# Two decoder blocks on one Trainium2 core: the modulation's matrix-vector product moves from TensorE to ScalarE and accumulating transfers, and the recurrence runs on two half buffers

## The reference, cut to what matters

```
c_act = jax.nn.silu(c)                                  # [1, 1024]
for l in range(2):
    mod = c_act @ w_ada[l] + b_ada[l]                   # w_ada[l]: [1024, 6144], 24 MB each
    sh_m, sc_m, gt_m, sh_f, sc_f, gt_f = jnp.split(mod, 6, axis=-1)
    h = rms_norm(x, g_mix[l]) * (1.0 + sc_m[:, None]) + sh_m[:, None]
    ...
```

## Time and profile before

| | us |
|---|---|
| median of 3 runs | 3211.62 (3207.85 to 3217.34) |
| the profiled execution, its own time | 3216.43 |
| its span in the profile | 3214.3 |
| TensorE busy | 2807.8 (87%) |
| VectorE busy | 1462.0 (45%) |
| ScalarE busy | 877.2 (27%) |
| GpSimd busy | 120.4 (4%) |

### The profile page before, as it was taken

The page is one execution under the profiler, slowest core; times in us unless marked ns, Lnnn a source line. Parts: engine busy times, 40 slices in busy tenths (PEclk is TensorE's granted clock), DMA queues, the critical chain, the costliest instruction groups (busy, mean ns, idle before and its releaser), DMA issues.

```text
span 3214.3 us, 48264 instructions
## 1 busy us (share of the span) xinstructions
PE 2807.8 (87%) x21116; PEld 2057.9 (64%) x21116; DVE 1462.0 (45%) x2707; ACT 877.2 (27%) x1416; POOL 120.4 (4%) x199
## 2 busy tenths in 40 slices
PE   6898989868896877875798899999998888999999
PEld 5686767646573332321676667888876666778887
DVE  5545444467453110102565646434455665554433
ACT  3312212132430000001233353322223334433221
POOL 0010101010000000000000000000000000000000
PEclk9999999978997998997899999999999999999999
DMA  4353534332128999997233332333332342323332
GB/s 145 115 173 100 166 100 149 97 124 107 47 91 354 428 427 428 427 428 289 68 86 102 70 118 86 92 98 94 97 84 82 91 87 86 105 80 97 99 98 79
DMA packets 151816, 489.57 MB, mean 152 GB/s; under 512 B 13232, under 2 KB 41488, under 8 KB 139184
## 3 DMA queue, kind: packets, MB, share of 16 engines
q1 hardware_dynamic: 112256, 362.37, 31.5%
q0 software_dynamic: 26384, 97.32, 9.2%
q10 hardware_dynamic: 12960, 26.74, 2.6%
HBM read 456.49 MB, written 29.90 MB: 151 GB/s over the span
## 4 chain that ended last, share of the span: by engine, by line
PE 67%; DVE 14%; DMA 12%; ACT 5%; issue 2%; SPq 0%; POOL 0%; DVEq 0%; ACTq 0%; POOLq 0%
PE psum L154 64%; DMA wslot<-in_w_up 4%; DMA wslot<-in_w_gate 3%; DMA wslot<-in_w_down 3%; PE psum L157 3%; DVE halfL L163 2%; DVE sc__235 L193 1%; ACT halfH L160 1%; DVE m L190 1%; DVE slot L163 1%; DVE a20S L178 1%; DVE a21S L178 1%; ACT a1S L160 1%; DVE US L163 1%; DMA ada<-in_w_ada 0%
## 5 line engine op out<-in xcount | busy, mean ns | idle before, releaser
L163 DVE TENSOR_TENSOR halfL<-ring,halfH 128x1024 fp32r<-128x1024 f32 x302 | 367.5, 1221 | 684.6 <-ACT halfH L160 684.5
L160 ACT ACTIVATE halfH<-ring 128x1024 fp32r<-128x1024 f32 x302 | 316.5, 1053 | 808.4 <-PE psum L154 808.2
L154 PE MATMUL psum<-hH,halfH 128*128 128x512 f32 x1200 | 486.3, 405 | 9.7 <-DVE halfL L163 9.6
L154 PE MATMUL psum<-hL,halfH 128*128 128x512 f32 x1200 | 473.4, 394 | 0.0
L154 PE MATMUL psum<-hH,halfL 128*128 128x512 f32 x1200 | 472.3, 394 | 0.0
L154 PE MATMUL psum<-wslot,XT 128*64 128x512 f32 x1024 | 258.8, 664 | 73.7 <-DMA wslot<-in_w_gate 42.7
L154 PEld LDWEIGHTS psum<-hH,halfH 128*128 128x128 f32 x1200 | 228.5, 190 | 83.9 <-issue 23.4
L154 PEld LDWEIGHTS psum<-hH,halfL 128*128 128x128 f32 x1200 | 228.5, 190 | 49.6
L154 PEld LDWEIGHTS psum<-hL,halfH 128*128 128x128 f32 x1200 | 229.1, 191 | 44.6
L154 PEld LDWEIGHTS psum<-wslot,XT 128*64 128x64 f32 x1024 | 90.3, 152 | 241.3 <-issue 235.5
L154 PE MATMUL psum<-halfH,hH 128*128 128x512 f32 (+2 forms) x576 | 219.8, 382 | 11.8 <-DVE halfL L163 8.4
(11 more groups left out here) (446 smaller groups left out, 3909.9 us busy)
## 6 DMA issues: line engine op xcount, KB each, us to landing
wslot<-in_w_gate SPq DMA_DIRECT2D x32, 2048.0 KB, 30.0
wslot<-in_w_up SPq DMA_DIRECT2D x32, 2048.0 KB, 28.9
wslot<-in_w_down SPq DMA_DIRECT2D x32, 2048.0 KB, 31.0
ring<-in_w_in SPq DMA_DIRECT2D x120, 512.0 KB, 3.8
ada<-in_w_ada POOLq DMA_DIRECT2D x96, 512.0 KB, 4.2
ring<-in_w_gu SPq DMA_DIRECT2D x88, 512.0 KB, 3.6
ring<-in_w_down SPq DMA_DIRECT2D x44, 512.0 KB, 3.8
gate_rows<-stage ACTq DMA_DIRECT2D x48, 256.0 KB, 2.1
```

Source lines behind the costliest of these rows:

```text
L154: return self.e.matmul(*a, **k)
L160: return self.e.activation(*a, **k)
L163: return self.e.tensor_tensor(*a, **k)
```

## The change

- A weight tile of the modulation is scaled by ScalarE (step `scaled`): row p times `cact[p, k]`. The first of a group (k = 0) goes to `ada_sum` (128 x 1024), the others stay in place.
- GpSimd issues for each of the seven other tiles of a group a transfer that adds the tile to `ada_sum` (84 in all). It waits for the last addition to have landed, issues load n + 2, waits for `scaled` n, and issues addition n. There are three buffers for the tiles.
- TensorE does only the sum over the partitions of the finished group: eight matmuls with a 128 x 128 piece of `ada_sum` as weights and one column of ones, which give `mods` in columns at once. ScalarE's copies to `arow` and the turning go.
- The steps stand elsewhere: per group eight `scaled`, an empty one and one `ada` (120 slots), one slot after each prep other than 1 to 4 and one at each loop step (35 slots a pair). The last group ends at prep 18 of pair 3.
- Two of the three tile buffers lie in the third half buffer. So the recurrence's woven products have two half buffers, splits go one tile ahead, and the first loads of the modulation wait for the last tile before the woven ones.
- The loads of `Zh` and the two gains move from GpSimd's queue to SyncE's, behind the loads of the woven tiles.

```diff
+    half_of, half_before = [], []
+    for n in range(len(tiles)):
+        half_of.append(n % 2 if FIRST_WOVEN <= n <= LAST_WOVEN else n % NH)
+        half_before.append(max([m for m in range(n) if half_of[m] == half_of[n]], default=None))
...
-    ada_in = [rk(f"ada{i}", 1024) for i in range(2)]
+    ada_sum, ada_in = rk("ada_sum", 1024), [rk("ada0", 1024)]
+    ada_in += [sb(f"ada{1 + i}", AT_HALF + 4096 + 1024 * i, 1024) for i in range(2)]
...
+    def ada_steps():
+        for g in range(12):
+            for k in range(8):
+                yield [("scaled", 8 * g + k)]
+            yield []
+            yield [("ada", g)]
...
-                if n_ada < 108:
-                    yield "ada", n_ada // 9, n_ada % 9
-                    n_ada += 1
+                if not 1 <= i < 5:
+                    yield from next(ada, [])
...
                 yield from next(woven, [])
+                yield from next(ada, [])
...
-        def rw_ada(g, k):
...
+        def rw_ada(g):
             b = bank(ADA_BANK)
+            clear(ADA_BANK)
+            pe.wait_ge(*at("ada_sum", 8 * g + 7))
+            for c in range(8):
+                i = pe.matmul(b[:, c:c + 1], ada_sum[:, c * 128:(c + 1) * 128], K("ones", 0, 1), start=True, stop=True)
+            i.then_inc(*up("ada_pe", "ada", g))
...
-                split_to(WOVEN[n][2].tiles[ti][0] + 2, LAST_WOVEN)
+                split_to(WOVEN[n][2].tiles[ti][0] + 1, LAST_WOVEN)
...
+        def rw_scaled(n):
+            ac.wait_ge(*at("cact"))
+            ac.wait_ge(*at("ada_in", n))
+            if n % 8 == 0 and n:
+                ac.wait_ge(*at("ada", n // 8 - 1))
+            ac.activation(ada_in[n % 3] if n % 8 else ada_sum, ada_in[n % 3], COPY,
+                          scale=cact[:, n % 8:n % 8 + 1]).then_inc(*up("ada_act", "scaled", n))
...
+        po.wait_ge(*at("tile", FIRST_WOVEN - 1))
+        for n in range(3):
+            ada_load(n)
         for n in range(96):
...
+            if n:
+                po.wait_ge(*(at("ada_sum", n - 1) if (n - 1) % 8 else at("scaled", n - 1)))
+                if n + 2 < 96:
+                    ada_load(n + 2)
+            po.wait_ge(*at("scaled", n))
+            if n % 8:
+                po.dma_start(ada_sum, ada_in[n % 3], accum_op=AD).then_inc(*landed("ada_sum", "ada_sum", n))
...
+        sp.wait_ge(*at("tile", LAST_WOVEN))
+        for i, who in enumerate(("q", "k")):
+            for ci in range(2):
+                for j in range(4):
+                    sp.wait_ge(*at("kept", who, ci, j))
+            sp.dma_start(Zh[who], z_rows.rearrange("(t p) n -> p t n", p=128)[:, :, 768 * i:768 * i + 768]
+                         ).then_inc(*landed(f"z_{who}", "z_in", who))
```

More of the change, by code:

```diff
@@ L273, in program @@
     t_pi = small("t_pi", 4, dt=I32)
-    arow = small("arow", 256)
     g8 = small("g8", 5)
@@ L325, in program @@
              for ci, ch in enumerate(chs)]
-    LAST_WOVEN = len(tiles) - 1
+    FIRST_WOVEN, LAST_WOVEN = G_q[0].tiles[0][0], len(tiles) - 1
     def merge_chunks(branches, wo):
@@ L589, in recurrence_order @@
     def recurrence_order():
-        n_ada, woven, heads = 0, woven_steps(), list(A1_HEADS)
+        woven, heads, ada = woven_steps(), list(A1_HEADS), ada_steps()
         for pr in range(4):
@@ L617, in recurrence_order @@
                 yield "normed", pr
-        assert not heads
+        assert not heads and next(ada, None) is None
     BETWEEN = {**{1 + i: ("norming", 3, i) for i in range(9)}, 12: ("gated", 3), 14: ("turned", 3)}
@@ L721, in gemm_bank @@
             n, k0, nk = ch.tiles[ti]
-            H, L = tile_view(halfH[n % NH], n), tile_view(halfL[n % NH], n)
+            H, L = tile_view(halfH[half_of[n]], n), tile_view(halfL[half_of[n]], n)
             n_out = ch.w // 128 if stay == "weights" else 4
@@ L1223, in split_to @@
                 ac.wait_ge(*at("tile_in", m))
-                if m >= NH:
-                    ac.wait_ge(*at("tile", m - NH))
-                ac.activation(tile_view(halfH[m % NH], m), tile_view(ring[m % NW], m),
+                if half_before[m] is not None:
+                    ac.wait_ge(*at("tile", half_before[m]))
+                ac.activation(tile_view(halfH[half_of[m]], m), tile_view(ring[m % NW], m),
                               COPY).then_inc(*up("split_act", "hsplit", m))
@@ L1541, in scalar_program @@
         ac.wait_ge(*at("us", 11))
-        handlers = {"head": rw_head, "prep": rw_prep, "normed": rw_normed, "turned": rw_turned, "ada": rw_ada,
+        handlers = {"head": rw_head, "prep": rw_prep, "normed": rw_normed, "turned": rw_turned, "scaled": rw_scaled,
                     "gemm": rw_gemm, "spill": rw_spill, "square": a1_square, "root": a1_root, "turn": a1_turn,
@@ L1576, in split_to @@
                 ve.wait_ge(*at("hsplit", m))
-                ve.tensor_tensor(tile_view(halfL[m % NH], m), tile_view(ring[m % NW], m),
-                                 tile_view(halfH[m % NH], m).bitcast(F32), SU).then_inc(*up("split_dve", "lsplit", m))
+                ve.tensor_tensor(tile_view(halfL[half_of[m]], m), tile_view(ring[m % NW], m),
+                                 tile_view(halfH[half_of[m]], m).bitcast(F32), SU).then_inc(*up("split_dve", "lsplit", m))
                 done[0] += 1
@@ L1834, in a1_turn, with rw_ada @@
             turned_out("a1", who, j, GEMM_BANKS[j % 4], *((qT, g8[:, 0:1]) if who == "q" else (kT, col("gqk", 1))))
[L1836 to L1841, removed]
+        def rw_ada(g):
+            ve.wait_ge(*at("ada", g))
+            ve.tensor_copy(mods[:, 8 * g:8 * g + 8], bank(ADA_BANK)[:, 0:8]).then_inc(*up("ada_dve", "mods", g))
         H_ = "hd_dve"
@@ L2302, in vector_program @@
         ve.wait_ge(*at("consts"))
-        ve.memset(arow, 0.0).then_inc(*up("ada_dve"))
         ve.memset(U[:, :, 0:514:513], 0.0).then_inc(*up(R_))
@@ L2371, in pool_program, with ada_load @@
         po.wait_ge(*at("n1", "turn", 7))
-        for n in range(96):
[L2373 to L2389, removed]
+        def ada_load(n):
+            L, part, k = n // 48, n // 8 % 6, n % 8
+            po.dma_start(ada_in[n % 3], T["w_ada_2"][L, k * 128:(k + 1) * 128,
+                                                     part * 1024:(part + 1) * 1024]).then_inc(*landed(f"ada{n % 3}",
+                                                                                                      "ada_in", n))
+        po.wait_ge(*at("tile", FIRST_WOVEN - 1))
+        for n in range(3):
+            ada_load(n)
+        for n in range(96):
+            if n:
[5 more added lines that the diff above has]
+                po.dma_start(ada_sum, ada_in[n % 3], accum_op=AD).then_inc(*landed("ada_sum", "ada_sum", n))
         po.wait_ge(*at(("a1", "q"), "turn", 5))
@@ L2502, in sync_program @@
             load(n)
+        sp.wait_ge(*at("tile", LAST_WOVEN))
[5 more added lines that the diff above has]
+                         ).then_inc(*landed(f"z_{who}", "z_in", who))
+        sp.dma_start(gqk_["q"], T["q_norm_g"].to_broadcast([128, 64])).then_inc(*landed("gqk"))
+        sp.dma_start(gqk_["k"], T["k_norm_g"].to_broadcast([128, 64])).then_inc(*landed("gqk", "gqk_in"))
         sp.wait_ge(*at("a1", "s", A1.n - 1))
```

## The result

The changed kernel takes 3463.7 us (median of 4 runs, 3460.2 to 3467.6), the one before 3210.0 us in the same comparison (4 runs): ratio 1.0786, 95% interval 1.0765 to 1.0808. It is slower by 7.9%; I had forecast slower, by 1.0%, in a range that ended at 3362.

What follows compares the result with a forecast made beforehand. The prediction took TensorE's order to bound the recurrence before, and the chain of additions after: its end at 758 us against 726 makes 32 us later, 3211.6 + 32 = 3243.6, said as 3244 us, range 3165 to 3362.

Steps and rivals of the forecast that it cites:

- the sum of the chain: GpSimd's additions in the recurrence: 137 + 12 x 44 + 84 + 9 = 758 us when the last group is summed.
- the landing X: Time from an adding transfer's issue on GpSimd's queue to its landing, taken as 5.0 us; break-even 4.6.
- the load ahead: What is left of the load in front of an addition in GpSimd's queue: 1.2 - 0.54 = 0.7 us.
- the restart: Between two groups of additions: TensorE's sum 2.1, two scalings 2.1 and signals 0.3, together 4.5 us.
- the holes: Stretches almost without slots from a loop's end to the next pair's prep 5: 28 us idle at each of three, 84.
- case A: Forecast, chance 0.45: the additions pace the recurrence, X between 4.7 and 6, 3220 to 3328 us, likeliest 3244.
- case C: Rival, chance 0.15: additions much slower than two reads, X from 6 on; 3370 us at 6.5, TensorE idle, clock lower.
- 84 links: Successive additions into one buffer, each 0.54 issue of the load, 5.0 landing and 0.1 to wake: 5.65 us.
- The wake: GpSimd's delay after each addition has landed, before its next instruction: about 0.1 us a link.
- The hidden gain: If every new transfer were hidden: 33 us less on TensorE plus 18 in pair 3 and waits, 51 us.
- The rule: Skill-based estimate of an addition's landing, 2.0 + 1.05 MB / 436 GB/s = 4.4 us; not adopted, sum 50 us lower.

## Why the prediction was wrong

The mechanism was right, and the sizes of its terms were not. The step that failed is the sum of the chain: first the landing X, in it the part for the load ahead (0.7 us taken, 1.8 measured), then the restart and the holes. The chain of additions paces the recurrence, TensorE waits at the sums and ScalarE at the scalings, and GpSimd's waits end by transfers. In sign and in cause this was case A. By its landing of 6.4 us it falls into case C (X from 6 on), and C's signs came too: TensorE idle for a third of the stretch and a lower granted clock. But C's reason was an addition that is slow by itself, and by itself it landed in 4.6 us. In size it was worse than the sum gives even at the X that was measured: 32 + 84 x (6.4 - 5.0) makes 150 us, and it was 254. I went through the chain of the changed kernel from 137 us to the end of its last sum at 975 us, by the terms of my sum, which ended at 758:

| | predicted | measured | difference |
|---|---|---|---|
| 84 links | 5.65 us each, 475 | 7.3 on average, 611 | +136 |
| restarts | 12 of 4.5 us, 54 | ten from 6.3 to 12.0, in sum 85, and the last sum, 4 | +35 |
| without an open link | 93 us | start 28, in pair 1 28, into pair 2 58, others 24 | +45 |

The 58 holds the eleventh restart, which fell into that hole.

**The landing.** X = 5.0 was put together from 3.1 for a copy, 1.2 for the second operand and 0.7 for the load ahead. The runs gave 3.1 for a copy with no load just ahead, 1.5 more for an addition in the same place, and 1.8 more with the load ahead. So the copy was right, and the largest miss is the load ahead: I had taken its time on the engines at the full rate of the transfers, less the 0.54 us between the issues. A load that lands 3.8 to 4.4 us after its issue was not out of the way so soon.

**The wake.** I took 0.1 us; the chain shows 0.28 after each landing, 84 x 0.18 = 15 us. With the 118 of the landing this is nearly all of the 136. Landings spread from 4.6 to 11.5 us; that the long ones, such as the 9.85 at 261.41, met the woven tiles' loads is my guess, and no run took these away.

**The restart.** I had summed TensorE's sum at full clock and two scalings back to back. The sum came behind a wait and at a lower clock (3.5 us, not 2.1), and only the first scaling may follow at once; the second stands in the next slot, behind a prep, a product and at times a split. With the steps moved together the restarts gave back 22 us of this.

**The holes.** I had assumed three open links at the start of each hole, and so 28 us idle in each. The hole into pair 2 had none:

```profile
605.55 0.90 POOL L196 DMA_DIRECT2D ada_sum<-ada  x1
612.40 0.55 POOL L196 DMA_DIRECT2D ada<-in_w_ada  x1 [5.96 <-DMA ada_sum<-ada]
643.64 0.53 POOL L196 DMA_DIRECT2D ada<-in_w_ada  x1 [30.70 <-ACT ada_sum L160]
669.73 0.88 POOL L196 DMA_DIRECT2D ada_sum<-ada  x1 [25.56 <-ACT ada L160]
```

The addition at 605.55 is the last of its group. Seven groups of ten slots fill two pairs of 35 slots exactly, so this group's sum is the last step of pair 1's loop, and the next group starts only behind the head. This could have been counted from the order of the steps.

**The hidden gain.** 51 us at best; 30 measured. The transfers' move gave its 11. TensorE's sums took 1.8 us each (I took 2.1), so its part should have been above 33. The half buffers took 11, for which I had 0 to 7 as a possible cost and nothing in the sum. Some 10 us of the difference are left. The loops of the run without additions are 6.5 us longer than before, which may be part of it; what lengthens them, scalings on ScalarE or the sums, stays open.

**The range.** I had made X the only unknown. The restart, the wake and the holes were terms too, and they all erred to the same side; the wake is multiplied by 84 and the restart by 12. The range ended at X = 6.4 with all else as summed; X came out at just that, and the time lay 102 us above the end.

**The rule.** The estimate of 4.4 us from the Trainium skill ("DMA: Bandwidth & Descriptors", Anatomy of one DMA, with "Collectives: The Full Stack", Part 3) would have put the sum 50 us lower. The runs stand close to it for an addition alone, 4.5 to 4.6 us, and far from it where it was needed: 6.4 us behind a load.

## What to carry to other kernels

Where each transfer adds into the same buffer and waits for the landing of the last, as here, the landings add up: 512 KB take 4.6 us alone and 6.4 beside the loads that feed them, while VectorE scales and adds the same tile in 1.3 us. Before a sum moves off an engine, multiply the whole link (landing, wake, what is queued in between) by the number of links and compare it with the time between the slots that hide it, here 3.2 to 3.6 us. Where a step is the end of a chain and the start of the next, list what stands between the two on every engine's queue: that is the restart, and here it was up to 12.0 us where the instructions alone gave 4.5. Count also where the groups of the chain end against the stretches without slots.

## What the runs showed of the hardware that I had not expected

- One transfer of 128 x 1024 float32 within the core's memory, issued by GpSimd: a copy lands in 3.1 us, an addition in 4.6; with a 512 KB load issued 0.53 us ahead 5.5 and 6.4; with it behind, 5.6 for the addition and 6.3 for the load.
- GpSimd is busy for 0.53 us with the issue of a copy, for 0.84 to 0.90 with that of an addition; its next instruction follows a landing by 0.28 us.
- GpSimd adds two tiles of 128 x 1024 float32 in 2.4 us, VectorE scales one and adds it in 1.28, ScalarE scales one by a column in 1.15.
- Beside an addition on GpSimd, VectorE instructions of 0.17 and 0.25 us lasted 2.35 and 1.12 us and ended with it, and splits 1.85 us on average in place of 1.22.
- TensorE's granted clock in 200 to 600 us is 0.81 with the waits for additions and 0.95 in the run without additions, and the short sum behind a wait took 3.5 us at 0.50, without a wait 1.85 us at 1.00.
